# Gated-linear heads of a two-layer streaming encoder: next head's projections inside the pair loop, whole-level vector operations, sub-block score matmuls

## The reference

```python
proj = h @ w_in                              # q, k, v, r of all heads
logf = log_sigmoid((h @ w_gate_a) @ w_gate_b + b_gate) / 16
b = cumsum(logf, axis=1)                     # within the chunk
inter = (q * exp(b)) @ s0
attn[l, m] = sum_k q[l,k] * k[m,k] * exp(b[l,k] - b[m,k])   # m <= l
o = inter + attn @ v
s_new = exp(b_last)[..., None] * s0 + (k * exp(b_last - b)).T @ v
# over all chunks, then: o * rsqrt(mean(o*o)) * g_onorm * silu(r), and @ w_out
```

## Time and profile before

| | us |
|---|---|
| median of 3 runs | 2792.67 (2791.11 to 2794.64) |
| the profiled execution, its own time | 2791.56 |
| its span | 2789.8 |
| TensorE busy | 2603.3 |
| VectorE busy | 1074.6 |
| ScalarE busy | 871.3 |
| GpSimd busy | 444.8 |

### The profile page before, as it was taken

How to read it: one execution, slowest core, us unless ns; L and a number is a source line. 1 busy time by engine, 2 the same in 40 slices (tenths; PEclk the granted TensorE clock), 3 DMA queues, 4 the chain that set the end, 5 groups by cost and what they waited for, 6 DMA issues and landing times.

```text
span 2789.8 us, 39379 instructions
## 1 busy us (share of the span) xinstructions
PE 2603.3 (93%) x15574; PEld 2484.8 (89%) x15574; DVE 1074.6 (39%) x2934; ACT 871.3 (31%) x1896; POOL 444.8 (16%) x187
## 2 busy tenths in 40 slices
PE   6789889889899999999998999989899999999997
PEld 5668778769799999999997988879899999999996
DVE  5455555462722222222228344451732222222227
ACT  4242423343512211211124466663522112211212
POOL 1011010111122112212211110101121122212210
PEclk9989899999899999999999999989999999999998
DMA  2000000002311111111113200000411111111113
GB/s 102 31 27 26 29 24 29 31 23 66 113 61 46 45 45 40 43 45 45 51 44 123 67 24 16 16 20 31 140 61 46 45 42 40 45 45 45 45 56 118
DMA packets 63085, 138.95 MB, mean 50 GB/s; under 512 B 8560, under 2 KB 39920, under 8 KB 62960
## 3 DMA queue, kind: packets, MB, share of 16 engines
q1 hardware_dynamic: 33984, 103.64, 11.2%
q10 hardware_dynamic: 28976, 33.64, 4.0%
HBM read 117.85 MB, written 19.40 MB: 49 GB/s over the span
## 4 chain that ended last, share of the span: by engine, by line
PE 79%; DVE 10%; ACT 3%; issue 2%; ACTq 0%; DMA 0%; POOL 0%; DVEq 0%
PE banks L201 56%; PE banks L181 12%; PE banks L1724 3%; PE banks L1256 2%; DVE gla_att L2221 1%; PE banks L1236 1%; PE banks L1247 1%; DVE gla_work L2203 1%; PE banks L1805 1%; DVE norm_acc_x L477 1%; DVE norm_acc L463 1%; DVE h_lo L548 1%; DVE y L524 1%; DVE gla_work L2204 1%; DVE gla_work L2188 1%
## 5 line engine op out<-in xcount | busy, mean ns | idle before, releaser
L158 POOL TENSOR_TENSOR w_lo<-w_raw,w_hi 128x1024 fp32r<-128x1024 f32 x180 | 441.4, 2456 | 2271.6 <-ACT w_hi L151 2271.6
L201 PE MATMUL banks<-h_hi,w_hi 128*128 128x384 f32 x1872 | 435.0, 341 | 38.9 <-ACT gla_vr L2106 31.3
L201 PE MATMUL banks<-h_lo,w_hi 128*128 128x384 f32 x1872 | 418.4, 332 | 0.0
L201 PE MATMUL banks<-h_hi,w_lo 128*128 128x384 f32 x1872 | 416.9, 331 | 0.0
L201 PEld LDWEIGHTS banks<-h_hi,w_hi 128*128 128x128 f32 x1872 | 320.3, 192 | 56.7 <-ACT gla_vr L2106 32.9
L151 ACT CAST w_hi<-w_raw 128x1024 fp32r<-128x1024 f32 x180 | 186.4, 1043 | 453.6 <-DMA w_raw<-in_units 453.2
L201 PEld LDWEIGHTS banks<-h_lo,w_hi 128*128 128x128 f32 x1872 | 323.7, 192 | 0.0
L201 PEld LDWEIGHTS banks<-h_hi,w_lo 128*128 128x128 f32 x1872 | 322.2, 191 | 0.0
L201 PE MATMUL banks<-mlp_a_hi,w_hi 128*128 128x384 f32 (+1 forms) x1344 | 296.6, 329 | 1.5 <-issue 1.3
L201 PE MATMUL banks<-mlp_a_hi,w_lo 128*128 128x384 f32 (+1 forms) x1344 | 295.1, 327 | 0.0
L201 PE MATMUL banks<-mlp_a_lo,w_hi 128*128 128x384 f32 (+1 forms) x1344 | 295.1, 327 | 0.0
(11 more groups left out here) (173 smaller groups left out, 3342.4 us busy)
## 6 DMA issues: line engine op xcount, KB each, us to landing
w_raw<-in_units SPq DMA_DIRECT2D x180, 512.0 KB, 3.3
x_scratch<-y ACTq DMA_DIRECT2D x48, 192.0 KB, 2.5
norm_x<-x_scratch ACTq DMA_DIRECT2D x48, 192.0 KB, 3.3
x_scratch<-y ACTq DMA_DIRECT2D x24, 160.0 KB, 1.8
norm_x<-x_scratch ACTq DMA_DIRECT2D x24, 160.0 KB, 2.9
y<-in_x SPq DMA_DIRECT2D x16, 192.0 KB, 5.0
norm_x<-in_x ACTq DMA_DIRECT2D x16, 192.0 KB, 3.4
out_y<-y SPq DMA_DIRECT2D x16, 192.0 KB, 2.8
```

The lines of the kernel that those rows point to most:

```text
L158: c.nc.gpsimd.tensor_tensor(c.w_lo[:, s], c.w_raw[:, s], c.w_hi[:, s].bitcast(F32), ALU.subtract).then_inc(self.ready, 1)
L201: mm = chip.nc.tensor.matmul(chip.banks[:, 3 * s + b, 0:WIDTH[b]], w, x[:, k, COLS[b]], start=(k == 0 and n == 0), stop=(k == n_k - 1 and ...
```

## The change

Every projection becomes a job that fills one PSUM bank (a block of k, q or r; a pair of v; a block of the gate; a turned half block of the previous head's output). `plan_jobs` cuts the jobs of a head into k-steps and deals them by columns over 27 slots, three per pair (18 for head 3), so the next head's gate, k, q (blocks 0 and 1) and six of nine v pairs are made in this head's pair loop and the rest at the next head's start. Jobs rotate over banks 0 to 3. r is copied raw and goes through silu once per head, in pair 0 of the next head. k and q of head h lie in two tiles of y, b and v_tok have two buffers.

The levels become (32, 16, 8, 4, 2), with a separate tile for neighbours in a pair of tokens. `differences` takes b - ref over all tokens of a level in one operation; ScalarE takes Abs of the five levels before a single Exp with scale -1/16. `decayed` is one multiplication for all query tiles and one for all key tiles. `scores` multiplies only sub-blocks, into one bank, and `attention` is three masked copies into a tile that was cleared once. The sums over chunks are two scans with a tile of resets. The output of a pair is made in the same pair, between its second and third slot. At the start, the gate of head 0 is ahead of the last k and q block; at the end, high and low parts of the first six tiles are made by blocks, in pairs 6 and 7 and behind the loop, and two early parts of the output projection stand in slots 23 and 25.

```diff
-    R_AT = ((0, 0, 0, 0, 0, 1, 2, 3, 5, 6, 7, 8, 9, 10, 11, 12), (0, 0, 1, 2, 3, 4, 5, 6, 8, 9, 10, 11, 12, 13, 14, 15))
...
+    LEVELS = (32, 16, 8, 4, 2)
...
+    LEAD = 3 * KT * BMAX
+    STEPS = (PARTS * NPAIR, PARTS * NPAIR, PARTS * NPAIR, 18)
+    GATE_AT = (1, 3, 3)
...
+    FILL_AT = (23, 25)
...
+    def jobs_of(self, h):
+        own = [("k", h, 2), ("q", h, 2)]
+        for j in range(NB):
+            own += [("turn", h - 1, 2 * j), ("turn", h - 1, 2 * j + 1), ("v", h, 2 * self.PER_BLOCK + j)]
+        r = [("r", h, i) for i in range(2 * NB)]
+        gate = [("gate", h + 1, b) for b in range(NB)]
+        coming = [(kind, h + 1, b) for b in range(2) for kind in ("k", "q")]
+        coming += [("v", h + 1, p) for p in range(2 * self.PER_BLOCK)]
+        return (own if h else []) + (gate + r + coming if h < GH - 1 else r)
...
+            lead = self.LEAD if h == 0 else 0
+            total = sum(s[2] for s in steps) - lead
+            slots, ends, done, slot = [[] for _ in range(self.PARTS * NPAIR + 1)], [[] for _ in range(self.PARTS * NPAIR + 1)], -lead, -1 if lead else 0
+            for job, k, columns in steps:
+                while slot < 0 <= done or slot >= 0 and done >= total * (slot + 1) / self.STEPS[h]:
+                    slot += 1
+                slots[slot].append((job, k))
+                done += columns
+                if k == (0 if job[0] in ("gate", "turn") else KT - 1):
+                    ends[slot].append(job)
...
+        def bank_ready(job):
+            n = self.at[job]
+            if n < JOB_BANKS:
+                if n < JOB_BANKS - 1:
+                    pe.wait_ge(self.start_taken, 3 * NB)
+                else:
+                    pe.wait_ge(self.v_copied, NPAIR)
+                return
+            previous = self.order[n - JOB_BANKS]
+            if previous[0] == "turn":
+                pe.wait_ge(self.o_gated, 2 * NB * previous[1] + previous[2] + 1)
+            else:
+                pe.wait_ge(self.job_taken, self.taken[previous])
...
-            for level in range(NLEV):
-                at = (level % 4) * P
-                nc.tensor.matmul(chip.banks[0:n, self.SCORE_BANK + level // 4, at:at + n],
-                                 w[:, level, 0:n], w[:, level, 0:n], start=True, stop=True)
...
+            for at, level in ((0, 5), (P, 4)):
+                s = self.LEVELS[level - 1]
+                split = lambda v: v.rearrange("p (n two s) -> p n two s", two=2, s=s)[:, :, 1]
+                for t in range(0, n, 32):
+                    nc.tensor.matmul(split(x[t:t + 32, at + t:at + t + 32]), e[:, level, t:t + 32],
+                                     split(qd[:, level, t:t + 32]), start=True, stop=True)
+            coarse = lambda t, m, q: x[t:t + m, P + q.start:P + q.stop]
+            for m in (8, 24):
+                for t in range(0, n, 32):
+                    q = slice(t + m, t + m + 8)
+                    nc.tensor.matmul(coarse(t, m, q), e[:, 3, t:t + m], qd[:, 3, q], start=True, stop=True)
+            for t in range(0, n, 32):
+                q = slice(t + 16, t + 32)
+                nc.tensor.matmul(coarse(t, 16, q), e[:, 2, t:t + 16], qd[:, 2, q], start=True, stop=True)
+            for t in range(0, n, CHUNK):
+                q = slice(t + 32, t + 64)
+                nc.tensor.matmul(coarse(t, 32, q), e[:, 1, t:t + 32], qd[:, 1, q], start=True, stop=True)
+            own = x[0:n, 2 * P:2 * P + n].rearrange("p (n two) -> p two n", two=2)
+            q = self.q_of(h)[:, t0:t0 + n].rearrange("p (n two) -> p two n", two=2)
+            nc.tensor.matmul(own[:, 0], self.k_of(h)[:, t0:t0 + n], q[:, 0], start=True, stop=True)
+            nc.tensor.matmul(own[:, 1], e[:, self.PAIR, 0:n], q[:, 1], start=True, stop=True
+                             ).then_inc(self.scores_full, 1)
...
+        fill(0, -1)
         for h in range(GH):
             for p in range(NPAIR):
                 scores(h, p)
+                fill(h, self.PARTS * p)
                 update(h, p)
+                fill(h, self.PARTS * p + 1)
+                output(h, p)
+                fill(h, self.PARTS * p + 2)
...
+            for job in self.ends[h][slot]:
+                kind, hd, i = job
+                if kind == "turn":
+                    continue
+                act.wait_ge(self.job_full, self.at[job] + 1)
+                bank = chip.banks[:, self.job_bank(job)]
...
+            nc.scalar.activation(self.vr[:], self.vr[:], ACT.Silu).then_inc(self.r_ready, 1)
...
+            nc.scalar.activation(e[:, 1:self.PAIR, 0:n], e[:, 1:self.PAIR, 0:n], ACT.Abs).then_inc(self.lev_abs, 1)
+            nc.scalar.activation(e[:, self.CW, 0:n], self.b[:, h % 2, t0:t0 + n], ACT.Exp, scale=1.0 / GATE_NORM)
+            act.wait_ge(self.lev_abs, g + 1)
+            nc.scalar.activation(e[:, 1:self.N_E, 0:n], e[:, 1:self.N_E, 0:n], ACT.Exp,
+                                 scale=-1.0 / GATE_NORM).then_inc(self.lev_exp, 1)
...
+                turned_key(h, p)
+                if h and p == 0:
+                    output_root(h)
+                    silu(h - 1)
+                    take_jobs(h, slot)
+                    scale_outputs(h, 0)
+                    level_exp(g + 2)
+                    scale_outputs(h, 1)
+                else:
+                    take_jobs(h, slot)
+                    level_exp(g + 2)
+                if slot in self.HIGHS[h]:
+                    ws.high(act, self.unit(h, self.HIGHS[h][slot]))
+                if h < GH - 1 and p == self.GATE_AT[h] + 1:
+                    gate_exps(h + 1)
+                if h < GH - 1 and p == self.GATE_AT[h] + 2:
+                    chunk_decays(h + 1)
...
+                take_jobs(h, slot + 1)
...
+                take_output(h, p)
+                if h and p == 0:
+                    scale_outputs(h, 2)
+                take_jobs(h, slot + 2)
...
+                if h == GH - 1 and p == 6:
+                    silu(h)
+                    early_high(0)
+                if h == GH - 1 and p == 7:
+                    early_high(1)
...
+            for t0, t1 in ((0, self.SCAN), (self.SCAN, T)):
+                op = nc.vector.tensor_tensor_scan(b[:, t0:t1], self.resets[:, 0:t1 - t0], self.flat[:, t0:t1], 0.0,
+                                                  ALU.mult, ALU.add)
+            op.then_inc(self.decay_sum, 1)
...
+            for i, s in enumerate(self.LEVELS):
+                groups = lambda x: x.rearrange("p (n w) -> p n w", w=2 * s)
+                nc.vector.tensor_tensor(groups(e[:, i + 1, 0:n]), groups(b),
+                                        groups(b)[:, :, s - 1:s].to_broadcast([P, n // (2 * s), 2 * s]), ALU.subtract)
+            for i, w in ((self.PAIR, 2), (self.END, CHUNK)):
+                groups = lambda x: x.rearrange("p (n w) -> p n w", w=w)
+                op = nc.vector.tensor_tensor(groups(e[:, i, 0:n]), groups(b),
+                                             groups(b)[:, :, w - 1:w].to_broadcast([P, n // w, w]), ALU.subtract)
+            op.then_inc(self.lev_diff, 1)
...
+            nc.vector.tensor_tensor(self.qd[:, g % 2, :, 0:n], e[:, 0:self.PAIR, 0:n],
+                                    self.q_of(h)[:, None, t].to_broadcast([P, self.PAIR, n]), ALU.mult).then_inc(self.qd_ready, 1)
+            dve.wait_ge(self.qd_ready, g + 1)
+            k = e[:, 1:self.N_E, 0:n]
+            nc.vector.tensor_tensor(k, k, self.k_of(h)[:, None, t].to_broadcast([P, self.N_E - 1, n]),
+                                    ALU.mult).then_inc(self.lev_ready, 1)
...
+            for i in range(3):
+                if i:
+                    dve.wait_ge(self.att_step, 2 * g + i)
+                elif g >= 2:
+                    dve.wait_ge(self.att_ready, g - 1)
+                nc.vector.copy_predicated(a, self.masks[0:n, i, 0:n], chip.banks[0:n, self.X_BANK, i * P:i * P + n]
+                                          ).then_inc(self.att_step if i < 2 else self.att_ready, 1)
...
+                attention(g)
+                if p == 0:
+                    nc.vector.memset(self.state[:, 0, 0], 0.0).then_inc(self.state_zero, 1)
+                    if h:
+                        output_variance(h)
+                decayed(g + 1)
+                if h and p == 0:
+                    output_inverse(h)
+                if h and p in (1, 2):
+                    gated(h - 1, 4 * p - 4)
+                    gated(h - 1, 4 * p - 3)
+                differences(g + 2)
                 states(h, p)
-                if h == GH - 1 and 5 <= p < 8:
-                    early_low(2 * p - 10)
-                    early_low(2 * p - 9)
-        inverse_rms(GH)
+                if h and p == 1:
+                    gated(h - 1, 2)
+                    gated(h - 1, 3)
+                if h < GH - 1 and p == self.GATE_AT[h]:
+                    gate_flat(h + 1)
+                if h < GH - 1 and p == self.GATE_AT[h] + 1:
+                    gate_sums(h + 1)
```

(76 more changed lines are left out.)

624 lines of the change are left out of this document (294 added, 330 removed).

## The result

The changed kernel takes 2726.5 us (2725.9 to 2727.7, four runs) against 2791.9 of the kernel before, run beside it: a ratio of 0.9772, with a 95% interval of 0.9749 to 0.9796. It is 65 us faster, where 39 were forecast, so the forecast was 26.5 us too slow. The profiled execution has a span of 2723.9 us.

The account below looks back on a forecast made before the run. TensorE was taken as the bound, with gaps in the pair loops where VectorE stands on the path. 107 + 259.4 + 151 + 41 = 558 against 604.3, 46 off, 7 given back, leaving 39: 2753 us, range 2718 to 2785.

Parts of the forecast that it names:

- step 2: Score matmuls of a pair: 44 small records at 45 ns, with the rest 2.54 us against 1.7 before.
- dense work: Projection matmuls dealt into the pair slots of the four heads: no column added, 259.4 us in all.
- 34 pairs of recurrence: Scores, update and outputs on TensorE: 4.45 us a pair, 37.8 a head, 151 us for four heads.
- waits, clock, the rest: TensorE's stalls in the four heads' loops, 41 us, plus 7 us for stretches at 1.2 GHz after stalls.
- The rival with cheap records: Small score records take 28 ns each: 25 us less, 2728 us; chance 0.16.
- The floor near 93 ns: Slower rival: a small score record has a floor near 93 ns, 72 us more, 2825 us; chance 0.11.
- 3. *VectorE.: VectorE's pair work: 5.6 us, not 7.1; 0.5 late in head 0, hidden in heads 1, 2 save two pairs.
- 4. *ScalarE.: ScalarE's pair list: Abs without table load, some 60 us a head, output copy 0 to 0.8 us late in head 0.
- 5 and 6. *Start and end.: Scores start at 107 instead of 114.5; the 14.3 us behind the last output stay as they are.
- the signs that I had named: Heads 1 to 2 248 us, TensorE busy over 90%, clock above 0.95, scores 2.5 us, last output 558 to 566.
- other engines set the pair: Rival: Abs with table loads, or bank evictions behind blocked output copies, give some 25 us back, 2778 us; chance 0.18.
- It does not do what it says: Rival: order kept, but new waits on TensorE's queue stall some 1.2 us a pair, 43 us, no change; chance 0.05.

Follow-up runs that it names:

- e6: Changed kernel with the 22 small score matmuls of each pair replaced by five full 128x128 ones, coarse levels' valid scores left out: 2731.4 us, ratio 0.9794.
- e11: Changed kernel with seven masked copies a pair instead of three, decayed left as two operations: 2755.6 us, ratio 0.9876.
- e7: Changed kernel with seven masked copies a pair instead of three and decayed as 6 + 7 operations of 128 columns: 2778.6 us, ratio 0.9965.
- e2: Changed kernel with the next head's three gate jobs behind the first two jobs of r in heads 1 and 2: 2715.4 us, ratio 0.9721.
- e4: Changed kernel with the next head's moved-up k, q and v all in one slot of the last pair: 2808.1 us, ratio 1.0056.
- e9: VectorE's states ahead of its differences, on top of the version with moved gate jobs, late cast and moved silu: 2728.5 us, ratio 0.9774.
- e5: Changed kernel with the 22 small score matmuls of each pair issued twice: 2735.9 us, ratio 0.9810.
- e8: Changed kernel with gate jobs behind two jobs of r, unit 27's cast in pair 8 and head 3's silu moved to pair 8: 2709.2 us, ratio 0.9709.

## Why the prediction came out as it did

The forecast's mechanism was right and its direction too. Its size was off by 26.5 us, and the term of the sum that was mis-sized is the one of step 2. The time lies in the stated range, and outside the 2738 to 2768 that the forecast gave itself. All terms for the loops, forecast and measured:

| term | forecast | measured |
|---|---|---|
| first scores | 107 | 108.0 |
| dense work | 259.4 | 259.4 (taken as forecast) |
| 34 pairs of recurrence | 151 | 34 x 3.02 = 102.7 |
| waits, clock, the rest | 41 + 7 | 66.4 |
| last output | 565 | 536.5 |

The 3.02 us are 1.18 (scores), 0.63, and 0.58 + 0.63 for the output; 66.4 is what is left to 536.5. So the recurrence was 48 us too dear and the rest 18 us too cheap.

1. *Dense work.* Neighbouring matmuls of 384 columns start 0.175 us apart, 0.46 ns a column, as assumed. Right.

2. *Score matmuls.* This is the mis-sized term. I took 45 ns a record, from halving 128x128 and 64x64 once more; the row gives 11.6, below even the lower bound of 28. Both rows that I scaled from use more of the array and more columns. The rival with cheap records names the right side; its 2728 us is close to the measured time by chance, since it took 25 us off where the records took 48 and the other terms gave 18 back. The floor near 93 ns did not show at all. The rule of the Trainium skill (TensorE: Matmul & The Clock Gate, "Part 3: Packing small matmuls") that weight loads overlap matmuls only when the row group differs, which I weighed, is against the measurement: by the 52 ns that I estimated with it the 44 records would last 2.3 us; they last 0.51. Sub-blocks are not where the time came from, though: replaced by full ones they give back 5 us (e6).

3. *VectorE.* Durations right, place wrong. I had it hidden in heads 1 and 2 outside two pairs. Adding 1.35 us to it costs 29 us (e11), adding copies and decayed 52 (e7). In pairs 3, 6, 7 and 8 of heads 1 and 2 it is indeed hidden; in pairs 0, 4 and 5, where it was to be covered, it is not, and these are the pairs with root and silu or the next head's gate in the lists. What I did not have: VectorE's differences feed `level_exp`, and `take_output`, for which the next scores wait, stands behind that in ScalarE's list, while the pair has become 1.36 us shorter by step 2. That the latter takes the room away is argued, not shown.

4. *ScalarE.* Abs loads no table in any of its 36 operations, as taken in the sum. The Trainium skill (ScalarE: Activation LUTs, "Table sets: the hidden batching unit") has abs in every set, and the trace agrees. TensorE's idle time in the four loops is 428.5 - 401.1 = 27.4 us, against 41 in the forecast. The clock takes more than the 7: 32.6 us of TensorE's busy time in the loops are at half clock, which costs 16 us, half of it in head 3, which I had as a stall. (The clock column would give 20, but it counts idle time at half clock too, 7 us in head 3's stretch of 506 to 523.) The other 23 us are neither; the first dense matmul behind the scores has its successor 0.26 us later instead of 0.175, and such seams between small and dense work were not in the sum, but that they are all of it is not shown. Two stalls I had not seen: the gate jobs' wait for banks (4.3 us a head with its half clock, e2) and the cast that waits for a slot (11.0 us in one wait on ScalarE, 1.95 of them on TensorE).

5 and 6. *Start and end.* 108.0 for 107, and 14.2 for 14.3. Right; only the two scans take 2.47 us, not 2.1.

Of the signs that I had named, head 1's first scores to head 2's last output take 232.2 us, not 248, with TensorE busy for 97% of it at a clock of 0.97; the last output ends at 536.5, not between 558 and 566.

The rival "other engines set the pair" had the releaser wrong, since evictions make only 1.9 us of waits of the dense matmuls (two, of the values' L1744), but it is ScalarE's list, worked through in order, that makes the 11.0 us of waits ahead of the scores. "It does not do what it says" is out.

The gain has two parts that need each other. Without the filling the kernel is slower than before (e4), without the shorter list of VectorE nearly as slow as before (e7). Their losses, 82 and 52 us, are not to be added: together they are more than twice the gain. Open: why the 0.75 us of `decayed` cost 0.9 of their amount and the 1.35 us of copies only 0.63, as they would if the copies first used up some slack, which is not shown; what lets the clock fall in some pairs and not in others with the same wait; and what the single silu per head is worth, since no run takes it back, though the 31.3 us of waits for it are gone from the list.

## What to carry to other kernels

To fill TensorE's gaps with dense work, give it one-bank jobs between the dependent steps; then what stands on VectorE and ScalarE between the scores and the next scores sets the length of every pair in which it is longer than TensorE's own work, and it must be shortened in the same change. When a kernel with waits gets slower, read the granted clock beside the idle time: in e9 it is the larger part of the loss. Put nothing into an in-order list (a cast, a table load, a job) whose releaser comes later than what stands behind it, and look whether a slot's "free" signal hangs on an instruction that is no longer there. Before you price a small matmul by scaling, time one: here it cost a quarter of the scaled value.

## What the runs showed of the hardware

- 44 fp32 records of 8 to 32 weight columns and 8 to 32 moving columns pass in 0.51 us, 11.6 ns each; doubled, all 88 pass in 0.89 us (e5). A 128x128 record stays at 112 ns.
- The granted clock is 0.50 in pairs without filling (163 to 190 us in e4), though the engine has an instruction under way for 72% of that time, and for 6.8 us around a gate wait of 0.9 us in the changed kernel; after the same wait it stays at 1.00 in e6. So filling pays twice: at e8's head 1 the clock is 1.00 and idle time 2.6 of 112 us.
- One operation over 896 columns takes 1.09 us where seven over 128 take 1.50; six over 128 take 1.29 against 0.95 for 768.
- In the changed kernel one VectorE operation over 768 columns took 2.60 us, from 120.82, while GpSimd's difference of a weight unit ran (120.23 to 122.60), and the two scans of head 2 took 4.52 us instead of 2.47 beside another (from 383.38).
